# A hybrid decoder step on one core: the four expert contributions of a token ranked by expert number, and added on two engines

## The chip, the cores and the metric

The kernel runs on one core of a Trainium2 chip. A core has TensorE (PE), VectorE (DVE), ScalarE (ACT), GpSimd (POOL) and SyncE (SP, which here only issues DMAs). The metric is device time in microseconds from start to end of one launch. Before the change it is 1570.39 us (median of three executions, 1568.65 to 1573.18).

## The reference, cut to what matters

One decoder layer is computed for 528 prompt rows (16 of them are meta tokens that are dropped at the end) and 8 sample rows: sparse attention, a pooling branch, a merge, and then a mixture of experts in float32. Only the last part matters here:

```python
logits = (x @ w_router) + b_router              # 520 rows, 32 experts
top_v, top_e = lax.top_k(logits, 4)
gates = softmax(top_v)
# for each of the 4 chosen experts of a row:
gu = x @ w_gu[e] + b_gu[e]                      # 1024 -> 2048
gate, up = min(gu[:, :1024], 7), clip(gu[:, 1024:], -7, 7)
y_e = ((up + 1) * gate * sigmoid(1.702 * gate)) @ w_down[e] + b_down[e]
out = x + sum over the 4 of gate_e * y_e        # then the final RMSNorm
```

## The kernel before, in words

The experts run one after another, 0 to 31, with up to 96 rows each (`CAP`; more rows go into further passes under an `If` on the largest count, which these inputs do not need). The weights, six loads of 2 MB per expert, stream from HBM through a ring of 2 MB slots in `weight_ring` (slots 0 to 5) and `ring_more`. For each expert PE computes gate and up in three rounds of 32 rows (`up`, `last_up`, line 1434), DVE and ACT turn each round into the activation (`group`: the bias is added at L1949, the two clamps are L1951 and L1952, ACT does the sigmoid at L947, the two products are L1955 and L1958, and L1961 transposes), and PE multiplies with the down weights (`down`, `last_down`, L1440 for rows 0 to 63, L1446 for the rest). ACT scales the result by the gate (`y_out`) and GpSimd scatters the rows by indirect DMA (L754) into `y_k` in HBM.

`y_k` holds four arrays of rows, one for each *rank*. Each of the 4 contributions of a token goes into the array of its rank, so that no two writes meet. The rank is a small number written into column 6 of `gx` by `choice_ranks` (from L1807); `pick` carries it to the slots, `keep` makes the row number of it. Before the change the rank is the place of the expert in the token's top-4 list, by logit. So any rank may occur for any expert, and each array is complete only when expert 30 is scattered. Expert 31 is not scattered: its slots are cleared (`last_rows` of GpSimd scatters zeros, semaphore `zeroed`), its output stays in SBUF in `y_last` (`y_kept` on ACT), and PE brings it to its tokens by a matmul with a 0/1 matrix `back` (L1584 to L1592, into PSUM `GB`).

The end, in the order of each engine:

- SP, `ranks_load`: waits for the last scatters, loads rank 0 into slot 2 (L576), then the four small sample loads (L572), then ranks 1 and 2 when PE has freed slots 3 and 4 (`gu_free`), then rank 3 in two halves (L579) into slot 5; `samples_back` (L583) follows.
- DVE: after the last `group` it makes the 16 additions of `add_rank` (L2029, 128x1024 each: 4 ranks by 4 row tiles; for rank 0 the kept rows `xn(t)` are the second input), with the 4 small ones for the sample rows (L2019) between rank 0 and rank 1. Rank k, tile m waits for rank k-1, tile m by the semaphore `dve_sum`.
- The final norm in five rows of tiles (`FIN_ORDER`): DVE adds `GB` (L2087), ACT squares and takes the root (L1012, L1014), DVE scales (L2076, L2077), SP writes out (L623).
- Each engine reads the count of the fullest expert (`value_load`) behind its last turn of the expert loop, and tests it in the `If` ahead of the final norm.

Of the kernel before, what the change touches and what calls it, by code (L numbers as in the profile page):

```python
# [34 lines left out]
NQ = NT - META  # L35
# [45 lines left out]
def build_step(nc, xT, xnat, consts, g_mix, w_mt, w_v, w_mix, pool_scale, w_bra, w_brp, w_out,  # L81
# [4 lines left out]
    with ctx:  # L86
# [133 lines left out]
        def xn(t):  # L220
            return part(QK, D * t, D) if t < 4 else part(X1, 4 * NT, D)
# [65 lines left out]
        def bank(n, w=512, at=0):  # L287
            return PSF[:, 512 * n + at:512 * n + at + w]
# [23 lines left out]
        wiT_in wi_moved wo_in wr_scaled wv_in xg_done xn_in xt_ready y_ready y_rest zero_late zi_set  # L312
        zq_done sample_turned zq_zero ztmp_in ys_in ys_step ys_back zeroed dve_sum""".split()
        S = {n: sem(n) for n in names}
# [45 lines left out]
        def _(sp):  # L360
# [224 lines left out]
            def ranks_load():  # L585

                sp.dma_start(ys[:, TOPE, :], x1_tail.rearrange("r (c x) -> (r c) x", x=64)).then_inc(S["ys_in"], 16)
                sp.wait_ge(scat[1], (NE // 2) * 16)
                sp.wait_ge(scat[0], (NE // 2 + 1) * 16)
                sp.wait_ge(S["zeroed"], 16)  # L590
                sp.wait_ge(S["down_done"], (NE - 1) * 2)
                rank_load(0)
                for k in range(TOPE):
                    sample_load(k)
                for k in range(1, TOPE):
                    sp.wait_ge(S["gu_free"], (NE - 1) * 3 + k)
                    rank_load(k)
                samples_back(1)

            def ranks_load_again():  # L600
# [8 lines left out]
                samples_back(2)  # L609

            sp.wait_ge(S["cnt_ready"], 1)
            most = sp.value_load(cnt_i[0:1, 0:1], min_val=0, max_val=NQ)
            ranks_load()
            with sp.If(CAP < most):
                sp.wait_ge(S["dve_sum"], SUMS)
                sp.wait_ge(S["ys_back"], 16)
                with sp.Fori(1, PASSES) as b:
                    with sp.If(b * CAP < most):
                        again(b)
                ranks_load_again()  # L620
# [7 lines left out]
        def _(po):  # L628
# [149 lines left out]
            def last_rows():  # L778
# [6 lines left out]
                scatter(0, scat[0])  # L785

            steps(0)
            po.wait_ge(S["cnt_ready"], 1)
            most = po.value_load(cnt_i[0:1, 0:1], min_val=0, max_val=NQ)
            last_rows()  # L790
            with po.If(CAP < most):
# [12 lines left out]
        def _(act):  # L804
# [189 lines left out]
            steps(0, True)  # L994
            act.wait_ge(S["cnt_ready"], 1)
            most = act.value_load(cnt_i[0:1, 0:1], min_val=0, max_val=NQ)
            y_out(0, NE - 2, 0, NE // 2 - 1, True)
            swish(0, NE - 1)
            y_kept(1)
            with act.If(CAP < most):  # L1000
                with act.Fori(1, PASSES) as b:
                    with act.If(b * CAP < most):
                        steps(b)
                        swish(b, NE - 1)
                        y_out(b, NE - 2, 0, NE // 2 - 1, False)
                        y_out(b, NE - 1, 1, NE // 2 - 1, False)
# [11 lines left out]
        def _(pe):  # L1018
# [541 lines left out]
            steps(0, True)  # L1560
            pe.wait_ge(S["cnt_ready"], 1)
            most = pe.value_load(cnt_i[0:1, 0:1], min_val=0, max_val=NQ)
            down(NE - 2, 0, (6, 2), ((NE // 2) * 16, (NE // 2 + 1) * 16))
            last_up()
            last_down()
            with pe.If(CAP < most):
                pe.wait_ge(S["y_rest"], 1)
                with pe.Fori(1, PASSES) as b:
                    with pe.If(b * CAP < most):
                        pick(b * NE + 1, 0, 0)  # L1570
                        pick(b * NE + 2, 1, 1)
                        steps(b)
                        up(b, NE - 1, 1, NE // 2 - 1)
                        down_in_turn(b, NE - 2, 0, False)
                        down_in_turn(b, NE - 1, 1, False)
                pe.wait_ge(S["all_added"], 1)
# [20 lines left out]
        def _(dve):  # L1597
# [207 lines left out]

            def choice_ranks(t0, t1):
                L(dve.scalar_tensor_tensor(out=rt_eg[:, t0:t1, 1, :], in0=rt_eq[:, t0:t1, 2, :], scalar=2.0, in1=rt_eq[:, t0:t1, 1, :],  # L1807
                                           op0=ALU.mult, op1=ALU.add))
                L(dve.scalar_tensor_tensor(out=gx[:, t0:t1, 0:NE, 6], in0=rt_eq[:, t0:t1, 3, :], scalar=3.0, in1=rt_eg[:, t0:t1, 1, :],
                                           op0=ALU.mult, op1=ALU.add))  # L1810

            for o, t in enumerate(WO_ORDER):
# [40 lines left out]
                for m in ((), (), (0,), (1,))[o]:  # L1853
                    find(m)
                    add_before(m)
                if o == 3:
                    choice_ranks(0, 1)
                    choice_ranks(4, 5)
            dve.wait_ge(S["rank_ready"], 1)
# [12 lines left out]
            def gates():  # L1872
# [3 lines left out]
                add_before(NTILE - 1)  # L1876
                choice_ranks(1, 4)
                slot_rows(2, 1, bank(FIRST_AT[1], 3, 400))
                dve.wait_ge(S["sel_ready"], 2)
                L(dve.tensor_reduce(sum4, rt_w, AX.X, ALU.add))  # L1880
# [139 lines left out]

            def add_rank(k, again):
                if k < 3:
                    dve.wait_ge(yk_full[k], 16 * (again + 1))
                for m, t in enumerate(FIN_ORDER[1:]):
                    if k == 3:
                        dve.wait_ge(y3_full[t // 2], 16 * (again + 1))
                    if k:
                        dve.wait_ge(S["dve_sum"], SUMS * again + 4 * k - 3 + m)
                    dve.tensor_tensor(yf[t], yf[t], yk[k][:, t, :] if k else xn(t), ALU.add).then_inc(S["dve_sum"], 1)  # L2029
# [3 lines left out]
            steps(0, True)  # L2033
            dve.wait_ge(S["cnt_ready"], 1)
            most = dve.value_load(cnt_i[0:1, 0:1], min_val=0, max_val=NQ)
            widen(NE - 1)
# [7 lines left out]
            group(NE - 1, 2, 1)  # L2044
            add_rank(0, 0)
            add_samples(0)
            for k in range(1, TOPE):
                add_rank(k, 0)
            with dve.If(CAP < most):
# [17 lines left out]
                for k in range(TOPE):  # L2067
                    add_rank(k, 1)
                dve.wait_ge(S["dve_sum"], 2 * SUMS)
                dve.wait_ge(S["ys_back"], 32)  # L2070
# [8 lines left out]
            for m, t in enumerate(FIN_ORDER):  # L2079
                r = TROWS[t]  # L2080
                if t == 4:
                    dve.wait_ge(S["ys_back"], 16)
                else:
                    dve.wait_ge(S["dve_sum"], SUMS - 4 + m)
                dve.wait_ge(S["gb_ready"], m + 1)
                y2 = yf[t][0:r].rearrange("p (a b) -> p a b", a=2)
                dve.tensor_tensor(y2, GB[m % 4][0:r], y2, ALU.add).then_inc(S["fin_gb"], 1)  # L2087
                if m:
                    fin_row(m - 1)
# [104 lines left out]
```

## Time and profile before

| what | us |
|---|---|
| median of three executions | 1570.39 |
| the profiled execution's own time | 1568.71 |
| its span, first to last instruction | 1567.0 |
| PE busy | 1535.2 (98%) |
| DVE busy | 792.5 (51%) |
| ACT busy | 259.8 (17%) |
| GpSimd busy | 189.7 (12%) |

The span is 1.7 us short of the execution's own time. PE is busy to 98%, so what can be won lies where PE stands still; the busy share of PE in the last of 40 slices is 5 tenths, and there the final additions and the norm lie. Durations are those of one profiled execution. All times of events are in us from the span's start.

### The profile page before, as it was taken

How to read it: one execution, taken by the hardware profiler on the slowest of the kernel's cores; microseconds unless marked ns; L12 is line 12 of the kernel's file. 1: busy time of each engine (PE TensorE's matmuls, PEld its weight loads, DVE VectorE, ACT ScalarE, POOL GpSimd, SP SyncE). 2: the span in 40 equal slices, each digit the busy share in tenths (PEclk: the TensorE clock that was granted, in tenths of full speed). 3: DMA queues.
4: the chain of work that ended last, by engine and by line, in shares of the span. 5: the costliest groups of instructions: out<-in, count | busy, mean ns of one | idle time of the engine just before them, and what ended most of it. 6: DMA issues, size and time to landing. Idle time of an engine off the chain costs nothing.

```text
span 1567.0 us, 33032 instructions
## 1 busy us (share of the span) xinstructions
PE 1535.2 (98%) x13237; PEld 720.6 (46%) x13237; DVE 792.5 (51%) x2042; ACT 259.8 (17%) x540; POOL 189.7 (12%) x266
## 2 busy tenths in 40 slices
PE   9999999999999999999999999999999999999995
PEld 7677487777755633333333333333333333333332
DVE  5349737704532654554455445544554455445528
ACT  2310030005401111111111111111111111111113
POOL 3633410014200000000000000000000000000000
PEclk9999999999999999999999999999999999999998
DMA  6455755723081679999999999999999999999995
GB/s 245 160 168 180 255 181 173 240 97 128 22 357 41 228 298 424 427 425 427 423 407 416 424 418 414 423 419 418 408 420 425 424 414 416 418 420 416 424 377 200
DMA packets 74494, 509.27 MB, mean 325 GB/s; under 512 B 15450, under 2 KB 15898, under 8 KB 49202
## 3 DMA queue, kind: packets, MB, share of 16 engines
q1 hardware_dynamic: 62298, 489.15, 77.2%
q0 software_dynamic: 12128, 19.23, 3.5%
q8 instruction: 40, 0.66, 0.2%
q14 instruction: 28, 0.23, 0.1%
HBM read 501.31 MB, written 23.68 MB: 335 GB/s over the span
## 4 chain that ended last, share of the span: by engine, by line
PE 94%; DVE 2%; issue 1%; ACT 1%; POOL 1%; DMA 1%; SPq 0%; DVEq 0%; POOLq 0%; ACTq 0%
PE PS L1434 42%; PE PS L1037 17%; PE PS L1440 14%; PE PS L1446 7%; PE PS L1345 4%; PE PS L1088 2%; PE PS L1153 2%; PE PS L1139 1%; PE PS L1203 1%; PE PS L1102 1%; DVE weight_ring L2029 1%; POOL weight_ring L717 1%; PE PS L1389 1%; PE PS L1248 1%; PE PS L1331 0%
## 5 line engine op out<-in xcount | busy, mean ns | idle before, releaser
L1434 PE MATMUL PS<-weight_ring,region_experts 128*32 128x512 f32 x5424 | 588.1, 592 | 0.9 <-ACT region_experts L941 0.9
L1434 PEld LDWEIGHTS PS<-weight_ring,region_experts 128*32 128x32 f32 x5424 | 177.4, 110 | 397.4 <-issue 393.6
L1940 DVE STREAM_TRANSPOSE region_experts<-region_x 32x256 f32<-32x256 f32 x372 | 161.8, 435 | 350.1 <-DMA region_x<-h_rows,idx_i 345.4
L1037 PE MATMUL PS<-region_x,region_w 128*128 128x260 f32 (+1 forms) x928 | 209.4, 385 | 1.0 <-DVE region_x L1722 1.0
L1037 PEld LDWEIGHTS PS<-region_x,region_w 128*128 128x128 f32 x928 | 175.2, 190 | 33.1 <-issue 4.6
L947 ACT ACTIVATE region_experts<-region_experts 128x256 f32<-128x256 f32 x96 | 40.0, 417 | 680.4 <-DVE region_experts L1951 680.4
L749 POOL DMA_INDIRECT region_x<-h_rows,idx_i x32 | 32.7, 1020 | 786.3 <-DVE idx_i L1926 687.5
L1440 PE MATMUL PS<-weight_ring,act_turned 128*32 128x512 f32 x992 | 112.5, 594 | 0.0
L1440 PE MATMUL PS<-weight_ring,region_x 128*32 128x512 f32 x992 | 112.5, 593 | 0.0
L1949 DVE TENSOR_TENSOR region_experts<-PS,region_w 128x512 f32<-128x512 f32 x96 | 64.0, 666 | 89.6 <-PE PS L1434 89.6
L1434 PE MATMUL PS<-ring_more,region_experts 128*32 128x512 f32 x720 | 80.0, 592 | 0.0
L1650 DVE MAX8 smalls<-weight_ring 8x8 f32<-8x1025 f32 (+4 forms) x96 | 71.6, 746 | 3.2
L956 ACT ACTIVATE region_x<-PS,smalls 64x512 f32<-64x512 f32 x62 | 42.4, 684 | 167.0 <-PE PS L1440 166.6
L1651 DVE MATCH_REPLACE8 weight_ring<-smalls,weight_ring 8x1025 f32<-8x1025 f32 (+4 forms) x96 | 69.9, 728 | 0.0
L960 ACT ACTIVATE region_x<-PS,smalls 32x256 f32<-32x256 f32 x124 | 57.7, 465 | 9.9 <-PE PS L1446 8.8
L1446 PE MATMUL PS<-weight_ring,region_x 128*32 128x256 f32 x992 | 59.2, 379 | 0.0
L1446 PE MATMUL PS<-weight_ring,act_turned 128*32 128x256 f32 x992 | 59.2, 379 | 0.0
L1440 PEld LDWEIGHTS PS<-weight_ring,region_x 128*32 128x32 f32 x992 | 31.0, 110 | 59.5 <-issue 56.1
L1955 DVE TENSOR_TENSOR region_experts<-region_experts 128x256 f32<-128x256 f32 x96 | 40.9, 426 | 33.8 <-ACT region_experts L947 33.8
L1440 PEld LDWEIGHTS PS<-weight_ring,act_turned 128*32 128x32 f32 x992 | 30.9, 110 | 58.4 <-issue 55.5
L754 POOL DMA_INDIRECT y_k<-region_x,idx_y x32 | 32.4, 1011 | 198.8 <-ACT region_x L960 162.4
L1345 PE MATMUL PS<-weight_ring,region_h 128*128 128x512 f32 x128 | 56.1, 595 | 0.0
(295 smaller groups left out, 1280.0 us busy)
## 6 DMA issues: line engine op xcount, KB each, us to landing
weight_ring<-w_gu SPq DMA_DIRECT2D x113, 2048.0 KB, 11.7
weight_ring<-w_down SPq DMA_DIRECT2D x62, 2048.0 KB, 11.8
ring_more<-w_gu SPq DMA_DIRECT2D x15, 2048.0 KB, 15.8
region_w<-w_mt SPq DMA_DIRECT2D x33, 512.0 KB, 4.5
weight_ring<-cache_kT SPq DMA_DIRECT2D x64, 256.0 KB, 4.1
weight_ring<-cache_v SPq DMA_DIRECT2D x64, 256.0 KB, 3.9
weight_ring<-y_k SPq DMA_DIRECT2D x3, 2048.0 KB, 12.2
weight_ring<-w_out SPq DMA_DIRECT2D x2, 2048.0 KB, 10.4
```

The source lines that it names most:

```text
L956: act.activation(ysc[u][0:64, 512 * h:512 * h + 512], bank(3)[64 * h:64 * h + 64], ACT.Copy, scale=gate_a[u][64 * h:64 * h + 64])
L960: ins = act.activation(ysc[u][64:CAP, QW * j:QW * j + QW], bank(4, QW)[GRP * j:GRP * j + GRP], ACT.Copy, scale=gate_b[u][GRP * j:GRP * j + ...
L1037: mm = pe.matmul(PB[j % 2][:, a, 0:width], lhs(k), rhs(k)[:, width * a:width * a + width], start=(k == 0), stop=(k == nk - 1))
L1345: mm = pe.matmul(PB[(J_WO + n) % 2][:, a, :], sga[:, k, rows_of(t)], wo[a][:, k, :], start=(k == 0), stop=(k == KD - 1))
L1434: mm = pe.matmul(bank(g)[GRP * q:GRP * q + GRP], hTe[u][:, k, GRP * g:GRP * g + GRP], w[:, k % 2, SEG * q:SEG * q + SEG], start=(k == 0), ...
L1440: mm = pe.matmul(bank(3)[GRP * j:GRP * j + GRP], actT[u][:, kk, GRP * g:GRP * g + GRP], w[:, kk % 4, 512 * h:512 * h + 512], start=(kk == ...
L1446: mm = pe.matmul(bank(4, QW)[GRP * j:GRP * j + GRP], actT[u][:, kk, 64:CAP], w[:, kk % 4, QW * j:QW * j + QW], start=(kk == 0), stop=(kk = ...
L1650: L(dve.max(out=max8[0:rows], in_=sc))
L1651: L(dve.match_replace(out=sc, in_to_replace=max8[0:rows], in_values=sc, imm_value=TAKEN))
L1940: ins = dve.transpose(hTe[u][32 * q:32 * q + 32, :, GRP * g:GRP * g + GRP], rows[GRP * g:GRP * g + GRP, :, 32 * q:32 * q + 32])
L1949: dve.tensor_tensor(gu, bank(g), b_wide, ALU.add).then_inc(S["biased"], 1)
L1955: dve.tensor_tensor(gu[:, 0:QW], gu[:, 0:QW], sg, ALU.mult).then_inc(S["gated"], 1)
```

## The change

Four things are changed.

1. The rank of a contribution becomes the number of the token's chosen experts with a lower index: an exclusive prefix sum of the 0/1 mask `rt_m` over the 32 experts, in five doubling steps on DVE (12 instructions; the old ranks took 3 times 2). It stands once in `gates`, behind `slot_rows(2, ...)`.
2. With it rank 0 can only come from experts 0 to 28, rank 1 from 1 to 29 and rank 2 from 2 to 30. SP loads rank 0 once expert 28 is scattered and PE is done with the down weights of expert 30, rank 1 once expert 29 is scattered and slot 3 is free, rank 2 once expert 30 is scattered and slot 4 is free; the zeros are awaited after that, then come the sample loads and rank 3.
3. GpSimd makes the additions of ranks 0 and 1, behind its last scatter; DVE makes those of rank 2, the samples, and rank 3. Rank 2, tile m waits for GpSimd's rank 1, tile m (`pool_sum`).
4. On all five engines the `value_load` of the count goes from behind `steps(0)` to right before the `If`.

```diff
             def ranks_load():
+                sp.wait_ge(scat[0], (NE // 2) * 16)
+                sp.wait_ge(S["down_done"], (NE - 1) * 2)
+                rank_load(0)
                 sp.dma_start(ys[:, TOPE, :], x1_tail...).then_inc(S["ys_in"], 16)
                 sp.wait_ge(scat[1], (NE // 2) * 16)
+                sp.wait_ge(S["gu_free"], (NE - 1) * 3 + 1)
+                rank_load(1)
                 sp.wait_ge(scat[0], (NE // 2 + 1) * 16)
+                sp.wait_ge(S["gu_free"], (NE - 1) * 3 + 2)
+                rank_load(2)
                 sp.wait_ge(S["zeroed"], 16)
-                sp.wait_ge(S["down_done"], (NE - 1) * 2)
-                rank_load(0)
                 for k in range(TOPE):
                     sample_load(k)
-                for k in range(1, TOPE):
-                    sp.wait_ge(S["gu_free"], (NE - 1) * 3 + k)
-                    rank_load(k)
+                sp.wait_ge(S["gu_free"], NE * 3)
+                rank_load(3)
                 samples_back(1)
...
+            def add_rank(k):                                    # GpSimd
+                po.wait_ge(yk_full[k], 16)
+                for m, t in enumerate(FIN_ORDER[1:]):
+                    if k:
+                        po.wait_ge(S["pool_sum"], 4 * k - 3 + m)
+                    po.tensor_tensor(yf[t], yf[t], yk[k][:, t, :] if k else xn(t), ALU.add).then_inc(S["pool_sum"], 1)
             steps(0)
+            last_rows()
+            add_rank(0)
+            add_rank(1)
             po.wait_ge(S["cnt_ready"], 1)
             most = po.value_load(cnt_i[0:1, 0:1], min_val=0, max_val=NQ)
-            last_rows()
...
-            def choice_ranks(t0, t1):                           # DVE, three calls
-                L(dve.scalar_tensor_tensor(... 2.0 ...))
-                L(dve.scalar_tensor_tensor(out=gx[:, t0:t1, 0:NE, 6], ... 3.0 ...))
+            def choice_ranks():                                 # DVE, one call
+                x, y = rt_eg[:, :, 1, :], rt_eg[:, :, 2, :]
+                L(dve.memset(rt_eg[:, :, 1:3, :], 0.0))
+                L(dve.tensor_copy(x[:, :, 1:NE], rt_m[:, :, 0:NE - 1]))
+                for shift in (1, 2, 4, 8, 16):
+                    dst = gx[:, :, 0:NE, 6] if shift == 16 else y
+                    dve.tensor_copy(dst[:, :, 0:shift], x[:, :, 0:shift])
+                    L(dve.tensor_tensor(dst[:, :, shift:NE], x[:, :, shift:NE], x[:, :, 0:NE - shift], ALU.add))
+                    x, y = y, x
...
             steps(0, True)                                      # DVE
-            dve.wait_ge(S["cnt_ready"], 1)
-            most = dve.value_load(cnt_i[0:1, 0:1], min_val=0, max_val=NQ)
...
-            add_rank(0, 0)
+            add_rank(2, 0)
             add_samples(0)
-            for k in range(1, TOPE):
-                add_rank(k, 0)
+            add_rank(3, 0)
+            dve.wait_ge(S["cnt_ready"], 1)
+            most = dve.value_load(cnt_i[0:1, 0:1], min_val=0, max_val=NQ)
             with dve.If(CAP < most):
...
             steps(0, True)                                      # PE
-            pe.wait_ge(S["cnt_ready"], 1)
-            most = pe.value_load(cnt_i[0:1, 0:1], min_val=0, max_val=NQ)
             down(NE - 2, 0, (6, 2), ((NE // 2) * 16, (NE // 2 + 1) * 16))
             last_up()
             last_down()
+            pe.wait_ge(S["cnt_ready"], 1)
+            most = pe.value_load(cnt_i[0:1, 0:1], min_val=0, max_val=NQ)
             with pe.If(CAP < most):
```

## Rows read from the trace of the kernel before

**Rows 1.** Timeline of PE and ACT: start, duration, instruction, count, [idle before it].
```profile
1495.38 1.90 ACT L960 ACTIVATE region_x<-PS,smalls 32x256 f32<-32x256 f32 x4 [0.27 <-PE PS L1446]
1497.38 3.64 PE L1440 MATMUL PS<-ring_more,act_turned 128*32 128x512 f32 x32 [2.06 <-issue]
...
1528.30 3.64 PE L1440 MATMUL PS<-weight_ring,region_x 128*32 128x512 f32 x32
...
1536.89 1.94 PE L1446 MATMUL PS<-ring_more,region_x 128*32 128x256 f32 x32
1544.27 1.86 PE L1584 MATMUL PS<-region_x 128*8 128x512 f32 x2 [5.44 <-issue]
1545.93 1.77 PE L1586 MATMUL PS<-region_x 128*8 128x512 f32 x2
```

**Rows 2.** Timeline of DVE from the end of the last expert on.
```profile
1536.01 1.00 DVE L2019 TENSOR_TENSOR region_x<-region_x 128x64 f32<-128x64 f32 x4
1536.92 13.71 DVE L2029 TENSOR_TENSOR weight_ring<-weight_ring 128x1024 f32<-128x1024 f32 x12
1550.55 1.21 DVE L2087 TENSOR_TENSOR region_w<-PS,region_w 8x1024 f32<-8x1024 f32 x1
```

**Rows 3.** Timeline of DVE in the last expert's rounds 0 and 1.
```profile
1523.28 0.43 DVE L1955 TENSOR_TENSOR region_experts<-region_experts 128x256 f32<-128x256 f32 x1 [0.36 <-ACT region_experts L947]
...
1525.86 0.29 DVE L1951 TENSOR_SCALAR region_experts<-region_experts 128x256 f32<-128x256 f32 x1
...
1527.69 0.45 DVE L1961 STREAM_TRANSPOSE region_x<-region_experts 128x256 f32<-128x256 f32 x1
```

**Rows 4.** Timeline of SP's DMA issues, 1500 to 1530.
```profile
1502.80 0.33 SPq L491 DMA_DIRECT2D ring_more<-w_down  x1
1503.96 0.57 SPq L587 DMA_DIRECT2D region_x<-x_tail  x1
1518.43 0.38 SPq L576 DMA_DIRECT2D weight_ring<-y_k  x1
...
1526.84 1.28 SPq L579 DMA_DIRECT2D weight_ring<-y_k  x2
```

**Rows 5.** The DMA issued at 1502.80: size, us from issue to landing.
```profile
ring_more<-w_down SPq DMA_DIRECT2D x1, 2048.0 KB, 14.5
```

**Rows 6.** Timeline of POOL: its last instruction before the change.
```profile
1512.95 0.98 POOL L754 DMA_INDIRECT y_k<-region_x,idx_y  x1 [0.30 <-issue]
```

**Rows 7.** Groups of POOL by line and form: count, busy us, mean ns of one.
```profile
L691 POOL TENSOR_TENSOR weight_ring<-weight_ring 128x528 f32<-128x528 f32 x10 | 10.9, 1090 | 36.3 <-ACT weight_ring L807 35.7
L717 POOL TENSOR_TENSOR weight_ring<-weight_ring 128x528 f32<-128x528 f32 x8 | 10.5, 1309 | 8.3 <-DVE smalls L1742 7.8
...
L717 POOL TENSOR_TENSOR weight_ring<-weight_ring 128x144 f32<-128x144 f32 x8 | 3.9, 493 | 6.7 <-DVE smalls L1742 6.4
```

**Rows 8.** Timelines of POOL and DVE where an addition and a copy overlap, and alone.
```profile
380.92 0.43 DVE L1715 COPY weight_ring<-smalls 128x512 f32<-128x512 f32 x1
...
399.65 2.17 POOL L717 TENSOR_TENSOR weight_ring<-weight_ring 128x400 f32<-128x400 f32 x2 [0.33 <-DVE smalls L1742]
...
401.23 0.87 DVE L1715 COPY weight_ring<-smalls 128x512 f32<-128x512 f32 x1
```

**Rows 9.** Busy time by stretch: PE, PEld, DVE, ACT, POOL, then PE clock, DMA share, GB/s.
```profile
1540.00:1542.00 2.00, 0.00 (x0) 0.00 (x0) 2.00 (x3) 1.97 (x3) 0.00 (x0) 1.00 0.79 281
...
1544.00:1546.00 2.00, 1.73 (x3) 0.33 (x4) 2.00 (x2) 0.00 (x0) 0.00 (x0) 0.50 0.03 8
1546.00:1548.00 2.00, 2.00 (x4) 0.36 (x3) 2.00 (x3) 0.00 (x0) 0.00 (x0) 0.65 0.01 4
```

**Rows 10.** Timelines of DVE and PE where the gates of the experts are made.
```profile
530.51 0.45 DVE L1887 TENSOR_TENSOR region_w<-region_w,choices 128x160 f32<-128x160 f32 x1
...
531.63 0.89 DVE L1889 TENSOR_TENSOR choices<-region_w,choices 128x160 bf16<-128x160 f32 x1
...
537.92 0.59 PE L1413 MATMUL PS<-choices,region_experts 128*96 128x4 bf16 x10
```

More of the change, by code:

```diff
@@ L312, in build_step @@
         wiT_in wi_moved wo_in wr_scaled wv_in xg_done xn_in xt_ready y_ready y_rest zero_late zi_set
-        zq_done sample_turned zq_zero ztmp_in ys_in ys_step ys_back zeroed dve_sum""".split()
+        zq_done sample_turned zq_zero ztmp_in ys_in ys_step ys_back zeroed dve_sum pool_sum""".split()
         S = {n: sem(n) for n in names}
@@ L609, in ranks_load_again @@
                 samples_back(2)
+            ranks_load()
             sp.wait_ge(S["cnt_ready"], 1)
             most = sp.value_load(cnt_i[0:1, 0:1], min_val=0, max_val=NQ)
-            ranks_load()
             with sp.If(CAP < most):
-                sp.wait_ge(S["dve_sum"], SUMS)
+                sp.wait_ge(S["dve_sum"], SUMS // 2)
                 sp.wait_ge(S["ys_back"], 16)
@@ L994, in _ @@
             steps(0, True)
-            act.wait_ge(S["cnt_ready"], 1)
-            most = act.value_load(cnt_i[0:1, 0:1], min_val=0, max_val=NQ)
             y_out(0, NE - 2, 0, NE // 2 - 1, True)
@@ L999, in _ @@
             y_kept(1)
+            act.wait_ge(S["cnt_ready"], 1)
+            most = act.value_load(cnt_i[0:1, 0:1], min_val=0, max_val=NQ)
             with act.If(CAP < most):
@@ L1804, in _ @@
             dve.wait_ge(S["xn_in"], 16 * NTILE)
-            def choice_ranks(t0, t1):
[L1807 to L1810, printed above, removed]
+            def choice_ranks():
[7 more added lines that the diff above has]
+                    x, y = y, x
             for o, t in enumerate(WO_ORDER):
@@ L1855, in _ @@
                     add_before(m)
-                if o == 3:
-                    choice_ranks(0, 1)
-                    choice_ranks(4, 5)
             dve.wait_ge(S["rank_ready"], 1)
@@ L1876, in gates @@
                 add_before(NTILE - 1)
-                choice_ranks(1, 4)
                 slot_rows(2, 1, bank(FIRST_AT[1], 3, 400))
+                choice_ranks()
                 dve.wait_ge(S["sel_ready"], 2)
@@ L2019, in add_samples, with add_rank @@
                     dve.tensor_tensor(ys[:, 0, :], ys[:, 0, :], ys[:, k + 1, :], ALU.add).then_inc(S["ys_step"], 1)
-            def add_rank(k, again):
+            def add_rank(k, again, tiles=(0, 1, 2, 3)):
                 if k < 3:
                     dve.wait_ge(yk_full[k], 16 * (again + 1))
-                for m, t in enumerate(FIN_ORDER[1:]):
+                for m in tiles:
+                    t = FIN_ORDER[1 + m]
                     if k == 3:
                         dve.wait_ge(y3_full[t // 2], 16 * (again + 1))
-                    if k:
-                        dve.wait_ge(S["dve_sum"], SUMS * again + 4 * k - 3 + m)
+                    if k == 2 and not again:
+                        dve.wait_ge(S["pool_sum"], 5 + m)
+                    elif k:
+                        dve.wait_ge(S["dve_sum"], 4 * k - 3 + m + (SUMS // 2 if again else -SUMS // 2))
                     dve.tensor_tensor(yf[t], yf[t], yk[k][:, t, :] if k else xn(t), ALU.add).then_inc(S["dve_sum"], 1)
@@ L2068, in _ @@
                     add_rank(k, 1)
-                dve.wait_ge(S["dve_sum"], 2 * SUMS)
+                dve.wait_ge(S["dve_sum"], SUMS + SUMS // 2)
                 dve.wait_ge(S["ys_back"], 32)
@@ L2083, in _ @@
                 else:
-                    dve.wait_ge(S["dve_sum"], SUMS - 4 + m)
+                    dve.wait_ge(S["dve_sum"], SUMS // 2 - 4 + m)
                 dve.wait_ge(S["gb_ready"], m + 1)
```

## The prediction, written before the result was known

> **What bounds the kernel now.** I read the page's busy times first: PE is busy for 98% of the span, so for the first 1539 us nothing counts that does not move PE. Then the timelines, engine by engine, of the last 60 us. PE begins the last down product at 1528.30 and ends it at 1538.83 (1536.89 + 1.94) [rows 1]. DVE makes its 16 additions from 1531.50 to 1550.6, without a gap: 12 of them take 13.71 us, so 1.14 each, and the four small ones 0.9 [rows 2]. At 1550.55 the first addition of the final norm starts, and the rest, 16.5 us up to the span's end at 1567.0, hangs on it. So from 1531.5 to 1550.6 DVE's additions set the end. Behind them stands a second path: PE's product for the kept rows starts at 1544.27 after 5.44 us in which it does nothing, and its first part ends at 1547.70 (1545.93 + 1.77) [rows 1]. The norm cannot start before that. Whatever is taken off DVE's additions, only 1550.55 - 1547.70 = 2.85 us are to be had until PE is late.
>
> All sums are in the profiled execution, whose own time is 1568.71 us. The median is 1.7 us above it; I add that at the end.
>
> **The ranks (12 DVE instructions).** They stand before the gates, whose last instruction ends at 532.52 (531.63 + 0.89), and PE first needs them at 537.92 [rows 10]: 5.4 us of cover. The neighbours of like size cost 0.45, and 0.89 where bf16 is written: at most 0.5 for the clearing, 9 x 0.45, 2 x 0.89, 6.3 us; the smallest shapes have 5 to 40 elements per partition, where 0.15 to 0.3 is likelier, so some 3.3. The old pair there (about 0.9 us) goes. Net 2.4, at most 5.4: hidden. The two removed pairs of the tile loop stood in idle time of DVE. Price 0, upper end 0.5. The number of rows scattered is the same.
>
> **The value loads.** PE's stood before the 2.06 us gap at 1497.38, but that gap ends when ACT has emptied the banks (1495.38 + 1.90 = 1497.28) [rows 1]: taking the load away there gives nothing. In its new place it stands alone. Its cost on PE is in no row; on SP the whole distance between two issues with a load between them is 0.83 us (1502.80 + 0.33 to 1503.96) [rows 4], so 0 to 0.83, and I take 0.8. DVE, ACT, SP and GpSimd have other work or slack there.
>
> **The loads.** Rank 0 is issued when PE ends expert 30 (10.5 us after 1497.38 [rows 1], as the last down product takes), 1507.9, not at 1518.43 [rows 4]. In front of it on the same queue is the 2 MB issued at 1502.80, which lands 14.5 us later, at 1517.3 [rows 5]. Another 2 MB at the some 420 GB/s of the page's slices of this stage takes 5.0 us, and the two last scatters of GpSimd (0.5 MB, 1 us), which before had an almost empty chip, run beside it. So rank 0 lands at 1522.4 to 1523.6. I take 1523.0. Rank 1 follows 5 us later. Rank 2 waits for the scatter issued at 1512.95 [rows 6], now under load, for which I take 11 us: 1524, landing by 1533. Rank 3 is issued at 1526.84 as before [rows 4] and lands by 1541. Nobody waits for ranks 1 to 3 in what follows. The weights of expert 31 stand ahead of rank 0 in the queue and are not delayed.
>
> **GpSimd's additions.** No row has 1024 columns. L717 gives 1309 ns for 528 and 493 for 144 columns, 2.125 ns per column [rows 7]: 1309 + 496 x 2.125 = 2.36 us. Lower end: by L691's 1090, 2.1. With 0.08 between two of them eight take 19.5 us, where DVE needed 9.1. GpSimd is free at 1513.9 [rows 6] and nothing else of GpSimd waits. Undisturbed: 1523.0 to 1542.5. Then DVE: the last addition of rank 2 (1.14), the samples (0.9), rank 3 (4.6): 1549.1, against 1550.6. That is all the change saves even when nothing collides: the loads come 10 us earlier, and the slower engine eats them.
>
> **The collision.** The eight additions now lie beside rounds 0 to 2 of the last expert, and PE waits for round 1 (the transpose ends at 1528.14, PE starts at 1528.30) [rows 3, 1]. What does a DVE instruction do beside a GpSimd addition? The copy of 128x512 takes 0.43 us alone. Started at 401.23, while an addition of GpSimd ran until 401.82 (399.65 + 2.17), it took 0.87, and ended 0.28 after it [rows 8]: it stood still until GpSimd was done, then ran at its own pace. The clamps L1951 and L1952 are of this kind (SBUF to SBUF, 256 columns in 0.29 us [rows 3]). For L1955 and L1958, which read two tensors from SBUF, no row overlaps a GpSimd addition. Bounds: 0, or the rest of one addition each (up to 2.36). The nearest row is the copy, so I take the wait. L1949 (one input in PSUM) and the transposes I leave undisturbed.
>
> The Trainium skill, "SBUF — State Buffer", section "Who interferes with whom", says that a VectorE instruction in a 2-port mode, or one with two SBUF inputs against a GpSimd instruction that reads SBUF, shares a port pair with GpSimd, and that the second to come blocks until the first is finished. By that rule the four waits of each round are all real; without its second half only the clamps wait, which is the first rival. The trace agrees for the copy (0.87 against 0.43); for two inputs no row here shows it.
>
> Step by step, rank 0 at 1523.0, GpSimd taking its turn after each DVE instruction: round 0, L1955 waits until 1525.4, L1958 until 1528.1, the transpose ends at 1529.0 (before: 1524.7). Round 1: L1949 until 1529.6, L1951 waits until 1530.9, L1952 until 1533.5, L1955 until 1536.0, L1958 until 1538.8, the transpose ends at 1539.7. PE starts the last down product at 1539.8, not at 1528.30: 11.5 later. If the second clamp slips through behind the first, 9.1; if rank 0 lands at 1522.4 and both clamps of round 0 are caught too, 16.
>
> PE then needs its 10.5 us. It has stood for 11 us; after its stand of 5.4 us the granted clock was 0.50 and 0.65 in the next two stretches [rows 9], that is the 1.2 GHz level for 3.4 us, and half of that is lost: 1.7. Then the stand before L1584: 5.44 before, while the rank loads still filled the DMA (share 0.79 at 1540 to 1542) [rows 9]. It stands at a branch over the code of the further passes. With the value load 6.2; with an empty DMA it may be shorter, down to the 1.1 us that ACT needs to deliver. I take 3.5. Then 3.4 to the end of its first part. Sum: 1539.8 + 10.5 + 1.7 + 3.5 + 3.4 = 1558.9, against 1550.55: +8.4. DVE's own additions end at 1556.1 by then (round 2 caught twice more, to 1546.0; then 4.6 + 0.9 + 4.6), so PE is the later. The rest is as before. 1568.71 + 8.4 = 1577.1, and with the 1.7 to the median **1579 us**. Its own range, by the bounds above (start of PE 9 to 16 later, stand 1.1 to 6.2), is 1573 to 1586.
>
> **Rivals.**
> - *Only the clamps wait.* For it: the only delayed row is a one-input instruction. Round 1 is then late by two waits, 4 us; PE starts at 1532.3, no clock is lost, 1532.3 + 10.5 + 4.5 + 3.4 = 1550.7; DVE's additions wait for GpSimd until 1543.5 and end at 1550.2. Against 1550.55: +0.2, with the median 1570.6.
> - *Nothing collides* (the other side: not slower). Its point is that neither kind of L1951 to L1958 waits. Then PE is as before: 1538.83 + 0.8 + 5.44 + 3.43 = 1548.5, the additions end at 1549.1: 1.4 earlier, 1569 us. Against it stands the copy's row.
> - *The ranks land early.* If rank 0 came at 1518 and PE's stand shrank to 2 us, additions end at 1544.1 and the kept rows at 1544.3 to 1545: 6 us earlier, 1564.5. Against it: the queue in front lands at 1517.3 [rows 5].
>
> **Chances.** The collision as forecast 0.64; only the clamps 0.12; nothing 0.19; early 0.05. A measurement of this kernel tells about 0.3% (4.7 us) from no change; slower is above 1575.1, faster below 1565.7. The collision's low end reaches into "same" by 0.03, the clamps' high end out of it by 0.02. So faster 0.05, same 0.32, slower 0.63. Range for 8 in 10: 1567 to 1586, which leaves out the early case, part of the third, and a collision dearer than all four waits.
>
> **What would show it.** Right: in rounds 0 and 1 of the last expert L1955 and L1958 take up to 2.8 us in the timeline, not 0.42; PE stands 9 to 16 us before the last L1440, with the clock at 0.5 behind it; GpSimd's L-row of additions has 8 of 2.4 us or more; rank 0 lands near 1523. Wrong: L1955 keeps 0.42 beside a running addition; or PE's 5.44 us stand does not shrink, or rank 0 lands by 1519.

## The result: 0.6% slower, and the profile after

The changed kernel takes 1579.89 us in the median of 8 runs (1574.88 to 1587.78); the kernel before, timed beside it on the same chip, takes 1571.35 (1568.65 to 1573.56, 8 runs). The ratio is 1.0057, with a 95% interval of 1.0035 to 1.0078. The profiled execution of the changed kernel took 1581.49 us, its span is 1579.7.

The timeline of the changed kernel from the last but one expert on, for DVE (VectorE), POOL (GpSimd) and PE (TensorE): start, duration, engine and line, instruction, count, [idle before it <-what ended it]. In the numbering after the change, L1964 adds the biases, L1966 and L1967 are the clamps, L1970 and L1973 the two products, L1976 the transpose, L796 GpSimd's additions, L2047 VectorE's, L2104 the first addition of the final norm.

```profile
1500.33 3.64 PE L1453 MATMUL PS<-ring_more,act_turned 128*32 128x512 f32 x32 [2.06 <-issue]
...
1524.64 0.69 DVE L1964 TENSOR_TENSOR region_experts<-PS,region_w 128x512 f32<-128x512 f32 x1 [11.84 <-PE PS L1447]
...
1526.00 9.73 POOL L796 TENSOR_TENSOR weight_ring<-weight_ring,region_qk 128x1024 f32<-128x1024 f32 x4 [9.44 <-DMA weight_ring<-y_k]
1526.22 2.43 DVE L1970 TENSOR_TENSOR region_experts<-region_experts 128x256 f32<-128x256 f32 x1 [0.36 <-ACT region_experts L960]
1528.76 2.42 DVE L1973 SCALAR_TENSOR_TENSOR region_experts<-region_experts 128x256 f32<-128x256 f32 x1
...
1532.26 1.27 DVE L1966 TENSOR_SCALAR region_experts<-region_experts 128x256 f32<-128x256 f32 x1
1533.45 2.42 DVE L1967 TENSOR_SCALAR region_experts<-region_experts 128x256 f32<-128x256 f32 x1
...
1535.69 9.73 POOL L796 TENSOR_TENSOR weight_ring<-weight_ring 128x1024 f32<-128x1024 f32 x4
1535.80 2.56 DVE L1970 TENSOR_TENSOR region_experts<-region_experts 128x256 f32<-128x256 f32 x1
1538.46 2.38 DVE L1973 SCALAR_TENSOR_TENSOR region_experts<-region_experts 128x256 f32<-128x256 f32 x1
...
1541.37 6.35 PE L1453 MATMUL PS<-weight_ring,region_x 128*32 128x512 f32 x32 [9.91 <-DVE region_x L1976]
...
1545.49 0.41 DVE L1970 TENSOR_TENSOR region_experts<-region_experts 128x256 f32<-128x256 f32 x1
...
1552.26 4.62 DVE L2047 TENSOR_TENSOR weight_ring<-weight_ring 128x1024 f32<-128x1024 f32 x4
...
1558.12 1.87 PE L1597 MATMUL PS<-region_x 128*8 128x512 f32 x2 [3.51 <-issue]
...
1561.80 1.21 DVE L2104 TENSOR_TENSOR region_w<-PS,region_w 8x1024 f32<-8x1024 f32 x1 [4.92 <-PE PS L1599]
...
1564.86 1.23 DVE L2104 TENSOR_TENSOR weight_ring<-PS,weight_ring 128x1024 f32<-128x1024 f32 x1 [1.84 <-PE PS L1605]
```

How to read it. GpSimd adds from 1526.00 to 1545.4, 2.43 us from start to start. Beside it, VectorE's products and second clamps take 2.4 to 2.6 us instead of 0.42 and 0.29 [rows 3]: each lasts one GpSimd addition. The two products of the third round come after GpSimd's end; the first, at 1545.49, takes 0.41 again. PE, which went straight on to the last down product at 1528.30 before [rows 1], now stands 9.91 us for the transpose of the second round. At the end it is PE and no longer VectorE that sets the norm's start: VectorE is done at 1556.9 and then waits 4.92 us.

The stretches of the same profile, with the columns of [rows 9]: span of the stretch, busy time and count of PE, PEld, DVE, ACT and POOL, then PE's granted clock, DMA share, GB/s.

```profile
1530.00:1536.00 6.00, 1.45 (x16) 0.27 (x8) 5.93 (x6) 0.42 (x1) 6.00 (x4) 1.00 1.05 400
1536.00:1542.00 6.00, 0.63 (x4) 0.20 (x8) 5.83 (x5) 0.00 (x0) 6.00 (x3) 0.55 0.64 263
1542.00:1546.00 4.00, 4.00 (x24) 0.99 (x20) 3.90 (x3) 0.42 (x1) 3.42 (x2) 0.50 0.00 0
1546.00:1550.00 4.00, 4.00 (x36) 1.04 (x32) 3.95 (x5) 0.00 (x0) 0.00 (x0) 0.89 0.00 0
```

PE stands still from 1531.5 to 1541.4. The granted clock falls within that stand (0.82 from 1536 to 1537, 0.50 from 1537 on), to the 1.2 GHz level, and stays there until about 1546.9. Some 5.5 of these 10 us lie over matmuls: the first 32 of the last down product take 6.35 us instead of 3.64, a loss of 2.7.

**Not all of the difference comes from the change.** The first bias addition of the last expert (L1949 before, L1964 after) starts at 1521.70 before, and at 1524.64 after, 2.94 us later, and GpSimd has not added anything by then. The shift is older than the new rank instructions too, which start at 529.54. Here is one addition of VectorE in the layers ahead, before and after:

```profile
450.76 0.42 DVE L1823 TENSOR_TENSOR region_x<-PS,region_x 8x256 f32<-8x256 f32 x1
```
```profile
453.87 0.42 DVE L1841 TENSOR_TENSOR region_x<-PS,region_x 8x256 f32<-8x256 f32 x1
```

In every profile below the first bias addition lies elsewhere, and PE's clock was at half speed for one stretch more or less in the layers ahead. All seven lie later than before, by 1.5 to 5.9 us. Of this, 1.6 to 3.1 us stand at this addition already; e_pool_rank0 and e_pool_last have one more stretch at half clock near 1502. So I compare profiles by the distances from this start to the norm's start, and from there to the span's end (in us):

| kernel | first bias addition | norm's start | distance | against before | from there to the end |
|---|---|---|---|---|---|
| before | 1521.70 | 1550.55 | 28.85 | | 16.5 |
| changed | 1524.64 | 1561.80 | 37.16 | +8.3 | 17.9 |
| e_dve_all | 1523.90 | 1552.74 | 28.84 | 0.0 | 16.5 |
| e_pool_clears (leaves additions out) | 1523.18 | 1546.44 | 23.26 | -5.6 | 16.8 |
| e_pool_later | 1523.27 | 1558.43 | 35.16 | +6.3 | 16.5 |
| e_quarters | 1524.62 | 1559.87 | 35.25 | +6.4 | 16.4 |
| e_pool_rank0 | 1527.44 | 1560.44 | 33.00 | +4.2 | 16.8 |
| e_pool_last | 1527.60 | 1565.67 | 38.07 | +9.2 | 16.4 |

### The profile page after: what moved, and what is told of

It is laid out like the page before. It is cut to its first block, busy times and chain, and to the rows that moved or that the text cites. A ratio compares the mean times of both kernels' runs of the same rounds, so it can differ in the third digit from the quotient of the medians.

```text
span 1579.7 us, 33040 instructions
## 1 busy us (share of the span) xinstructions
PE 1542.7 (98%) x13237; PEld 721.4 (46%) x13237; DVE 798.5 (51%) x2040; ACT 259.7 (16%) x540; POOL 208.7 (13%) x274
## 4 chain that ended last, share of the span: by engine, by line
PE 95%; DVE 2%; issue 1%; POOL 1%; ACT 1%; DMA 1%; SPq 0%; DVEq 0%; POOLq 0%; ACTq 0%
PE PS L1447 41%; PE PS L1050 16%; PE PS L1453 14%; PE PS L1459 7%; PE PS L1358 4%; PE PS L1101 2%; PE PS L1166 2%; PE PS L1152 1%; PE PS L1216 1%; PE PS L1115 1%; POOL weight_ring L721 1%; PE PS L1402 1%; PE PS L1344 0%; PE PS L1261 0%; PE PS L1283 0%
## 5 line engine op out<-in xcount | busy, mean ns | idle before, releaser
L1964 DVE TENSOR_TENSOR region_experts<-PS,region_w 128x512 f32<-128x512 f32 x96 | 63.8, 665 | 87.5 <-PE PS L1447 87.5
L1970 DVE TENSOR_TENSOR region_experts<-region_experts 128x256 f32<-128x256 f32 x96 | 45.0, 468 | 33.2 <-ACT region_experts L960 33.2
```

The source lines that it names most:

```text
L1964: dve.tensor_tensor(gu, bank(g), b_wide, ALU.add).then_inc(S["biased"], 1)
L1970: dve.tensor_tensor(gu[:, 0:QW], gu[:, 0:QW], sg, ALU.mult).then_inc(S["gated"], 1)
```

## The experiments

Each is the changed kernel with one edit; the short names are those of the table.

**e_dve_all: everything early as in the change, but no work on GpSimd.**

```
-            add_rank(0)                     # GpSimd
-            add_rank(1)
...
-            add_rank(2, 0)                  # VectorE
+            add_rank(0, 0)
             add_samples(0)
-            add_rank(3, 0)
+            for k in range(1, TOPE):
+                add_rank(k, 0)
```

> The changed kernel (new ranks, early loads, value loads before the If), but VectorE makes all 16 additions after its last round, GpSimd none. Theory (GpSimd's additions hold VectorE's clamps and products up, and nothing else of the change costs): L1970 and L1973 take 0.42 us again, PE starts the last down product 0.2 us after round 1's transpose, 17.6 us after it began the last expert's gate and up products (not 30.7), the final norm starts as in the kernel before or up to 0.5 us later; ratio to before 0.998 to 1.002. Rival (the early loads, the new ranks or the moved value loads cost): the ratio stays at 1.004 to 1.006 with no GpSimd addition in the trace.

Measured: 1573.08 us against 1570.34, ratio 1.0012 (0.9996 to 1.0028). The timelines of DVE and PE in its profile:

```profile
1528.90 0.42 DVE L1968 TENSOR_TENSOR region_experts<-region_experts 128x256 f32<-128x256 f32 x1 [0.35 <-ACT region_experts L958]
...
1539.12 13.70 DVE L2043 TENSOR_TENSOR weight_ring<-weight_ring 128x1024 f32<-128x1024 f32 x12
1552.74 1.21 DVE L2101 TENSOR_TENSOR region_w<-PS,region_w 8x1024 f32<-8x1024 f32 x1
```
```profile
1530.50 3.64 PE L1451 MATMUL PS<-weight_ring,region_x 128*32 128x512 f32 x32
...
1546.25 1.86 PE L1595 MATMUL PS<-region_x 128*8 128x512 f32 x2 [5.22 <-issue]
```

With the ranks' new instructions, the early loads and the late value loads in place, the products take 0.42 us, PE starts the last down product without a wait, and VectorE's 16 additions end where they did. Everything in the change but GpSimd's additions costs nothing that can be told (the interval ends at 0.3%), and gains nothing either: VectorE could not use the data earlier, since it was busy with the rounds until the same moment. The 17.6 us in the expectation is a slip: from the last expert's first matmul to the last down product it is 20.6 us here and before (1528.30 - 1507.70).

**e_pool_clears: GpSimd writes where it added.**

```
-                    po.tensor_tensor(yf[t], yf[t], yk[k][:, t, :] if k else xn(t), ALU.add)...
+                    po.memset(yf[t], 0.0)...
```

> The changed kernel, but GpSimd clears the eight tiles (128x1024 each) instead of adding, so ranks 0 and 1 and the kept rows are left out of the output; the waits are the same. GpSimd then writes SBUF and reads none, about 0.95 us each. Theory by the Trainium skill, SBUF - State Buffer (a two-input VectorE instruction meets only a GpSimd instruction that reads): beside a clear L1970 and L1973 take 0.42 us, while the clamps L1966 and L1967 wait up to 1 us. Rival (any GpSimd instruction on SBUF blocks both kinds): L1970 and L1973 take up to 1.4 us too. Rival (only one is affected by reads and writes alike): neither waits. Time 1566 to 1572.

This kernel leaves out eight additions; it is there for its waits, not for its time. Measured: one run, 1564.89 us, below the 1566 to 1572 expected. The timeline where GpSimd's clears lie beside the three rounds:

```profile
1524.95 3.63 POOL L796 MEMSET weight_ring<- 128x1024 f32 x4 [9.92 <-DMA weight_ring<-y_k]
...
1525.29 0.42 DVE L1973 SCALAR_TENSOR_TENSOR region_experts<-region_experts 128x256 f32<-128x256 f32 x1
...
1527.34 1.39 DVE L1966 TENSOR_SCALAR region_experts<-region_experts 128x256 f32<-128x256 f32 x1
...
1530.15 3.92 POOL L796 MEMSET weight_ring<- 128x1024 f32 x4 [1.57 <-DMA weight_ring<-y_k]
...
1532.07 1.11 DVE L1967 TENSOR_SCALAR region_experts<-region_experts 128x256 f32<-128x256 f32 x1
...
1533.10 0.41 DVE L1970 TENSOR_TENSOR region_experts<-region_experts 128x256 f32<-128x256 f32 x1
1533.61 0.42 DVE L1973 SCALAR_TENSOR_TENSOR region_experts<-region_experts 128x256 f32<-128x256 f32 x1
```

This separates the two kinds of instruction on VectorE. The clamps, with one input, are held by a GpSimd instruction that only writes (1.39 and 1.11 us instead of 0.29). The products, with two, are not: they take 0.41 and 0.42 while the last clear runs until 1534.07, and 0.42 at 1525.29 beside the first clears. They were held in the changed kernel, where GpSimd reads. So the products' wait does not come from GpSimd's being busy. The clears are also shorter than the additions, 0.9 against 2.4 us. That this is not the reason is shown by the next experiment, whose GpSimd instructions read and are shorter still (0.75 us): there the products are held.

**e_quarters: each of GpSimd's additions in four of 128x256.**

```
-                    po.tensor_tensor(yf[t], yf[t], yk[k][:, t, :] ..., ALU.add)...
+                    for q in range(4):
+                        ...
+                        c = slice(256 * q, 256 * q + 256)
+                        po.tensor_tensor(yf[t][:, c], yf[t][:, c], (yk[k][:, t, :] ...)[:, c], ALU.add)...
```

> The changed kernel, but each GpSimd addition is cut into four of 128x256 (0.73 us each by 188 + 256 x 2.125 ns; 32 of them, 26 us). Theory (the wait lasts to the end of the GpSimd instruction in flight, which takes turns with VectorE's): no clamp or product in rounds 0 to 2 takes over 1.3 us, PE starts the last down product 4 to 6 us late instead of 13, GpSimd ends 26 to 33 us after rank 0 landed, and the end is 5 to 11 us later than before because of GpSimd's length. Rival (the two share the bandwidth of a port): the waits add up to the same in both cuts, and PE is late by 10 to 13 us as in the changed kernel.

Measured: one run, 1578.02 us. Its timeline (here L1969 is the second clamp, L1972 and L1975 the products):

```profile
1527.33 12.02 POOL L798 TENSOR_TENSOR weight_ring<-weight_ring,region_qk 128x256 f32<-128x256 f32 x16 [10.81 <-DMA weight_ring<-y_k]
...
1530.27 0.95 DVE L1972 TENSOR_TENSOR region_experts<-region_experts 128x256 f32<-128x256 f32 x1
1531.32 0.76 DVE L1975 SCALAR_TENSOR_TENSOR region_experts<-region_experts 128x256 f32<-128x256 f32 x1
...
1532.62 3.64 PE L1455 MATMUL PS<-weight_ring,region_x 128*32 128x512 f32 x32 [1.19 <-DVE region_x L1978]
...
1539.32 13.92 POOL L798 TENSOR_TENSOR weight_ring<-weight_ring 128x256 f32<-128x256 f32 x16
```

A wait lasts to the end of the GpSimd instruction in flight: with additions of 0.75 us (12.02 / 16) a product takes 0.76 to 0.95, not 2.4. PE waits 1.19 us instead of 9.91 and starts the last down product 1.4 us late (4 to 6 expected), and its clock does not fall over the down product. Not all of that comes from the quarters: GpSimd started 2.71 us after the first bias addition here, 1.36 in the changed kernel, and so missed the first round. The second round is held throughout in both. From its bias addition to its transpose's end it takes 3.0 us undisturbed, 4.5 here and 9.7 in the changed kernel. So the quarters cut the loss in a fully held round from 6.7 us to 1.5. The rival, in which the waits add up to the same in both cuts, falls by this. Yet the norm is 6.4 us late. Quartering moved the loss: GpSimd now needs 25.9 us (12.02 + 13.92) for its eight tiles, and VectorE's additions wait for them.

**e_pool_later: GpSimd starts after the second round.**

```
+            po.wait_ge(S["actT_ready"], (NE - 1) * ROUNDS + 2)
             add_rank(0)
```

> The changed kernel, but GpSimd waits with its additions until the transpose of round 1 of the last expert is done. Theory: rounds 0 and 1 are undisturbed, PE's last down product starts on time, only round 2 is held up (which PE awaits 7 us later); GpSimd ends 19.5 to 21 us after round 1 (1528.2 + 20 = 1548 in the times of the kernel before), VectorE's additions end 6.6 us behind it at 1554 to 1556, against 1550.6: 4 to 5 us slower than before, ratio 1.002 to 1.004. Rival (GpSimd's place does not matter, its slow additions alone are the cost): about as slow as the changed kernel, 1.005 to 1.008, since its additions end even later.

Measured: 1578.26 us, ratio 1.0048 (1.0034 to 1.0062), above the 1.002 to 1.004 that was expected and close to the rival's 1.005. By the time alone, the rival (GpSimd's place does not matter) is not excluded. Its timeline:

```profile
1529.87 3.64 PE L1454 MATMUL PS<-weight_ring,region_x 128*32 128x512 f32 x32
...
1539.41 11.44 POOL L796 TENSOR_TENSOR weight_ring<-weight_ring 128x1024 f32<-128x1024 f32 x4
...
1540.26 1.93 PE L1460 MATMUL PS<-weight_ring,region_x 128*32 128x256 f32 x32 [3.31 <-DVE region_x L1977]
...
1542.05 11.01 DVE L2048 TENSOR_TENSOR weight_ring<-weight_ring 128x1024 f32<-128x1024 f32 x4 [1.85 <-POOL weight_ring L796]
...
1558.43 1.20 DVE L2105 TENSOR_TENSOR region_w<-PS,region_w 8x1024 f32<-8x1024 f32 x1
```

PE starts the last down product on time and waits 3.31 us in its middle, for the third round, with no fall of the clock (1.00 in every stretch from 1520 to 1558). Still 6.3 us are lost: VectorE's four additions of rank 2 take 11.01 us beside GpSimd's, where four alone take 4.6, and GpSimd's four take 11.44 instead of 9.73. I had priced the wait for GpSimd's results and left out that the additions then hold each other up. So the rival was right that moving GpSimd gains little, but the loss is another: in the changed kernel it is PE's wait, here it is the additions.

**e_pool_last: GpSimd starts when the last round is done.**

```
+            po.wait_ge(S["actT_ready"], NE * ROUNDS)
             add_rank(0)
```

> The changed kernel, but GpSimd's eight additions start only after the transpose of the last round. Both theories: the rounds take 0.42 us products and TensorE starts the last down product on time, so its clock and its wait are as before. Theory (the two engines' additions exclude each other): VectorE's additions of rank 2 stand between GpSimd's of rank 1, each pair some 3.6 us, so that GpSimd's second four take about 13 to 14 us instead of 9.7 and the norm starts about 10.5 us later than before: ratio 1.0067, between 1.005 and 1.008. Rival (VectorE only waits for the data, and both engines run beside each other): GpSimd's eight take 19.5 us, norm 7 us later, ratio 1.0046, between 1.0035 and 1.005, with VectorE's additions at about 1.15 us from start to start wherever their data is there.

Measured: 1581.57 us against 1571.09, ratio 1.0054 (1.0036 to 1.0071), the norm 9.2 us late (expected 10.5, the rival 7). The ratio's interval holds both the theory's 1.005 to 1.008 and the rival's 1.0046, so the profile has to decide. The profile's rows for GpSimd's line (durations in ns, least, median and most; first and last start), and VectorE's additions of rank 2 in the timeline:

```profile
L796 POOL TENSOR_TENSOR weight_ring<-weight_ring,region_qk x4: 2327/2374/2377, 1537.6 to 1544.6; 128x1024 f32<-128x1024 f32 x4
L796 POOL TENSOR_TENSOR weight_ring<-weight_ring x4: 2328/2825/3324, 1546.9 to 1554.8; 128x1024 f32<-128x1024 f32 x4
```
```profile
1549.32 10.98 DVE L2048 TENSOR_TENSOR weight_ring<-weight_ring 128x1024 f32<-128x1024 f32 x4 [11.84 <-POOL weight_ring L796]
1560.22 0.99 DVE L2035 TENSOR_TENSOR region_x<-region_x 128x64 f32<-128x64 f32 x4
```

Alone, GpSimd's addition takes 2.33 to 2.38 us. With VectorE's beside it, it takes up to 3.32, and VectorE's up to 3.36 instead of 1.2. The last of VectorE's four meets none and takes 1.2 us; the other three start 3.26 us apart ((10.98 - 1.21) / 3), near the 2.35 + 1.14 = 3.5 that one after the other would need: they take turns. The rival, in which both run at their own pace, would have had VectorE at 1.14 from start to start. The rounds are untouched in this kernel and PE starts on time, and it is as slow as the changed one. So keeping GpSimd out of the rounds does not save the idea.

**e_pool_rank0: GpSimd adds only rank 0.**

```
             add_rank(0)                     # GpSimd
-            add_rank(1)
...
+            add_rank(1, 0)                  # VectorE
+            add_samples(0)
             add_rank(2, 0)
-            add_samples(0)
             add_rank(3, 0)
```

> The changed kernel, but GpSimd adds only rank 0 to the kept rows (4 additions) and VectorE makes the other 12. Theory (VectorE's instructions wait out GpSimd's, and what counts is how far GpSimd's work reaches into the three rounds): the four additions lie from about 1526 to 1535.7 us as in the changed kernel, so the second round is held as there (products of about 2.4 us) but the third is free (0.42 us); the last transpose ends about 5 us sooner than in the changed kernel, TensorE's wait before the last down product falls from 9.9 us to about 5, VectorE then has 13 us of additions and the norm starts about 2.5 us later than in the kernel before, the start of the run set aside: ratio 1.0016, between 1.0005 and 1.003. Rival (the damage is in proportion to GpSimd's time): half of the changed kernel's 1.0057, 1.0028, with products in the third round slow too. Rival (the first collision costs it all): as the changed kernel, 1.005.

Measured: 1573.41 us against 1571.09, ratio 1.0006 (0.9992 to 1.0021), within the expected range; both rivals (1.0028 and 1.005) lie outside the interval. Its timeline:

```profile
1527.02 9.63 POOL L796 TENSOR_TENSOR weight_ring<-weight_ring,region_qk 128x1024 f32<-128x1024 f32 x4 [9.48 <-DMA weight_ring<-y_k]
...
1531.85 2.60 DVE L1969 TENSOR_TENSOR region_experts<-region_experts 128x256 f32<-128x256 f32 x1
...
1538.87 0.42 DVE L1969 TENSOR_TENSOR region_experts<-region_experts 128x256 f32<-128x256 f32 x1 [0.35 <-ACT region_experts L959]
...
1548.53 9.16 DVE L2046 TENSOR_TENSOR weight_ring<-weight_ring 128x1024 f32<-128x1024 f32 x8
1560.44 1.21 DVE L2104 TENSOR_TENSOR region_w<-PS,region_w 8x1024 f32<-8x1024 f32 x1 [2.74 <-PE PS L1598]
```
```profile
1540.36 6.62 PE L1452 MATMUL PS<-weight_ring,region_x 128*32 128x512 f32 x32 [6.11 <-DVE region_x L1975]
```

Here the first bias addition was late (1527.44), so GpSimd caught exactly the first round: its clamps and products are held, and those of the next two rounds are free. VectorE's additions end 30.25 us after the first bias addition, only 1.3 more than before; but PE waited 6.11, ran 32 matmuls in 6.62 us instead of 3.64, and the norm waits for PE. It is 4.2 us late, more than the 2.5 expected; the 32 matmuls at half clock alone cost PE 3.0 us. This profile belongs to the slowest of the kernel's ten runs (1578.89; the others 1569.59 to 1577.85), so it shows the mechanism and not the typical price. That a short reach into the rounds costs little is shown by the ratio; how often PE's clock falls in the other runs is open.

No version here that makes all additions beats the kernel before: the nearest are this one and e_dve_all, and neither can be told from it.

## Why the prediction was right, step by step

The forecast was 1579 us and slower; 1579.89 was measured. Times of the changed kernel in this list, from "Rank 0's landing" on, have 2.94 taken off; those of the first item are as the trace has them.

- **The ranks are hidden.** Right. From the clearing at 529.54 to the last addition's end at 532.62 they take 3.1 us (estimated 3.3), and PE's product over the gates still starts without a wait:

```profile
529.54 0.33 DVE L1822 MEMSET region_w<- 128x320 f32 x1
...
532.02 0.60 DVE L1827 TENSOR_TENSOR choices<-region_w 128x80 bf16<-128x80 f32 x1
```
```profile
540.86 0.59 PE L1426 MATMUL PS<-choices,region_experts 128*96 128x4 bf16 x10
```

- **Rank 0's landing.** Issued at 1508.0 (1507.9 forecast), GpSimd starts on it at 1523.1 (1523.0). That the queue in front of it decides fits this; no run tests it.
- **GpSimd's addition.** 2.43 us from start to start against 2.44 (2.36 and 0.08), worked out from two widths of another line [rows 7]. Undisturbed it is 2.34 (9.36 for four in e_pool_last), so the forecast for one alone was 0.1 too high, and VectorE's instructions beside it made up for that.
- **The collision.** Right in kind: all four instructions of a round wait, and the products as long as the copy's row [rows 8] had suggested. PE starts the last down product at 1538.4 (1539.8). The Trainium skill, "SBUF — State Buffer", section "Who interferes with whom", gave the rule before there was a row for two inputs; both halves of it are now measured here. The changed kernel shows the products held by a reading instruction, the clears show them free beside one that only writes. The first rival (clamps alone wait, 1570.6) fell by the products' rows. The range's lower end, 1573, is about 1 us below what the bounds named for it give (1579 - 2.4 - 2.4 = 1574.2).
- **PE's clock.** Right in kind, too small. The forecast was 3.4 us at half clock and 1.7 lost, from the stand before [rows 9]; it was some 10 us at half clock, the first 4 to 5 of them during the stand itself, and 2.7 lost. A second fall came at the stand at the branch, as before the change, but it lasted 6.8 us instead of 3.4, and now VectorE waits for PE: the second tile waited 1.84 us, and the tail is 17.9 instead of 16.5. The prediction had PE as the later of the two and still took the rest "as before". In e_pool_clears and e_pool_rank0, where PE is the later too but is at full clock by then, the second tile waits 0.70 and the tail is 16.8. So 0.3 of the 1.4 comes from PE being last and 1.1 from the clock. These are two terms of the sum that were mis-sized, +1.0 and +1.4; a third, PE's start, was 1.4 too late.
- **The stand at the branch.** 3.51 us against a forecast of 3.5, of bounds 1.1 to 6.2. The reason given (the DMA is empty by then) fits all profiles, though no run changes the DMA alone. The DMA share over PE's last 2 us before the stand is 1.03 before and 0.57 in e_dve_all, and the stands are 5.44 and 5.22; it is 0.03 to 0.16 in the other six, and the stands are 3.05 to 3.60. ACT is not what PE waits for: before, its last copy of the kept rows ends at 1540.80, and PE starts at 1544.27. The value load's 0.8 is not seen: e_dve_all has the load in the stand and the kernel before has not, and its stand is no longer.
- **The sum.** Norm's start 1558.9 forecast, 1558.86 measured. This agreement is better than its parts: PE started 1.4 earlier and lost 1.0 more to the clock, and small differences make up the rest. The time of the profiled execution (1581.49) is above the forecast of 1577.1 by the 2.94 before the rounds and the 1.4 of the tail, and the median of the runs is 1.6 below it. That 1579.89 lies so near 1579 is therefore in part luck: the forecast left out these 4.4 us, but it also put the median 1.7 above the profiled execution, and it lies 1.6 below; the two cancel to within 1.1. Of the medians, 1579.89 - 1571.35 = 8.5 us, the forecast was 8.4.
- **The chances.** The ratio's whole interval lies above 1.003, as 0.63 had said. Where the range was thin is its upper end: single runs reached 1587.8. The runs' mean clocks fall as their times rise, from 0.991 at 1574.9 to 0.985 at 1587.8, as would follow if more of these runs have a fall of PE's clock; that it is the collision that varies was not tried. It has room to vary: GpSimd's start lies from 0.4 us ahead of the first bias addition (e_pool_rank0) to 2.7 behind it (e_quarters), and how many of VectorE's instructions are held depends on that.

## What to carry to other kernels

VectorE and GpSimd are not two engines for elementwise work in SBUF with two inputs: their additions take turns, and GpSimd's turn costs 2.4 us where VectorE's costs 1.1 (128x1024, float32), so every addition handed over lengthens the sum of both wherever VectorE has work beside it. No run put GpSimd's additions where VectorE stands idle, as it does for 11.5 us ahead of the last expert's first round, so that case is not shown. Before moving work to an "idle" GpSimd, ask what VectorE does in that time, and who waits for VectorE: here a chain of 0.3 and 0.4 us instructions, on which PE waits, paid one GpSimd instruction each. Cutting GpSimd's instructions short protects such a chain (a fully held round loses 1.5 us instead of 6.7) but makes GpSimd slower (19.5 to 25.9 us for all); data that arrives early is worth nothing while the engine that uses it is the bound.

## What the runs showed of the hardware that was not expected

- GpSimd's clears cost VectorE's clamps up to 1.1 us each, and its products nothing; its additions cost both. The difference was expected, its cleanness was not: 0.41 to 0.42 us for every product beside a clear.
- GpSimd nearly kept its pace in the changed kernel (9.73 us for four additions, with products, clamps and transposes of 0.3 to 0.65 us between them; 9.36 undisturbed in e_pool_last), but lost 1 us on each addition that met one of VectorE's of 1.14 us.
- Waits of PE of 9.9 and 6.1 us were followed by half clock over the next 32 matmuls (6.35 and 6.62 us instead of 3.64), waits of 3.3 and 1.2 us were not. The length of a wait does not settle it alone: of the stands at the branch, those of 3.05 (e_pool_rank0), 3.51 (changed), 3.40 (e_quarters) and 3.60 us (e_pool_last) had half clock in or right behind them, those of 3.15 (e_pool_clears) and 3.24 us (e_pool_later) had not.
- The first bias addition differs by up to 4.4 us between profiles of the changed kernel and its variants, which are equal up to there. Of two profiled executions alone, +12.7 us of span would have been read as the price; 2.94 of it lay ahead of GpSimd's additions, and as much already ahead of the new ranks.
